# A two-layer transformer kernel: weight columns streamed through TensorE from last to first

## What is computed

```python
# first block
z = rmsnorm(x, attn_norm_g) @ w_in
x = x + concatenate([y_pool, y_attn], -1) @ w_out
up = rmsnorm(x, ffn_norm_g) @ w_up          # 2048 x 11264, then the convolution
x = x + (silu(gate) * val) @ w_down         # 5632 x 2048
# second block
proj = rmsnorm_2(h, attn_norm) @ w_in
qh = rmsnorm_2(c_q, q_norm) @ w_uq;  kv = rmsnorm_2(c_kv, kv_norm) @ w_ukv
mixed = g_a * (y_a @ w_branch_a) + g_b * (y_b @ w_branch_b)
h = h + mixed @ w_out
h = h + (silu(hn @ w_gate) * (hn @ w_up)) @ w_down
return rmsnorm_2(h, final_norm)
```

## Time and profile before

| | |
|---|---|
| median of 3 runs | 2428.22 us |
| the profiled execution | 2428.58 us |
| its span in the profile | 2426.7 us |
| TensorE matmul, busy | 2417.1 us, 11684 instructions |
| TensorE weight load, busy | 2036.5 us |
| VectorE, busy | 1371.2 us |
| ScalarE, busy | 1178.5 us |
| read from memory | 446.02 MB, 185 GB/s over the span |

### The profile page before, as it was taken

The page is one execution under the profiler, slowest core; times in us unless marked ns, Lnnn a source line. Parts: engine busy times, 40 slices in busy tenths (PEclk is TensorE's granted clock), DMA queues, the critical chain, the costliest instruction groups (busy, mean ns, idle before and its releaser), DMA issues.

```text
span 2426.7 us, 31051 instructions
## 1 busy us (share of the span) xinstructions
PE 2417.1 (100%) x11684; PEld 2036.5 (84%) x11684; DVE 1371.2 (57%) x1594; ACT 1178.5 (49%) x1534; POOL 59.8 (2%) x100
## 2 busy tenths in 40 slices
PE   9999999999999999999999999999999999999998
PEld 8788888888888888888888888888888888888887
DVE  5675456777777765445454454665545445454544
ACT  5544445555555544445455544544444444444443
POOL 0000000000000000001120000000000000000000
PEclk9999999999999999999999999999999999999999
DMA  7665456666666655556655556556666666666664
GB/s 249 176 178 167 148 183 182 192 186 185 192 192 179 195 196 190 190 190 186 186 165 174 162 160 184 189 184 189 187 189 188 190 190 189 189 190 207 193 193 155
DMA packets 241049, 449.40 MB, mean 185 GB/s; under 512 B 20100, under 2 KB 26980, under 8 KB 240832
## 3 DMA queue, kind: packets, MB, share of 16 engines
q1 hardware_dynamic: 239952, 445.57, 60.4%
q0 software_dynamic: 624, 2.24, 0.3%
q10 hardware_dynamic: 384, 0.37, 0.0%
HBM read 446.02 MB, written 2.10 MB: 185 GB/s over the span
## 4 chain that ended last, share of the span: by engine, by line
PE 99%; issue 0%; DMA 0%; DVE 0%; ACT 0%; POOLq 0%; POOL 0%; ACTq 0%; DVEq 0%
PE acc L576 25%; PE acc L578 25%; PE acc L577 25%; PE acc L925 7%; PE bank L925 7%; PE bank L928 3%; PE acc L928 3%; PE bank L567 2%; PE bank L749 1%; PE bank L777 0%; PE bank L807 0%; PE bank L726 0%; PE bank L778 0%; PE bank L752 0%; DMA stage<-in_gains 0%
## 5 line engine op out<-in xcount | busy, mean ns | idle before, releaser
L1350 DVE TENSOR_TENSOR w_lo<-w_raw,w_hi 128x1024 fp32r<-128x1024 f32 (+1 forms) x843 | 1027.6, 1221 | 1019.4 <-ACT w_hi L1015 1018.7
L1015 ACT ACTIVATE w_hi<-w_raw 128x1024 fp32r<-128x1024 f32 (+1 forms) x843 | 887.2, 1055 | 1110.9 <-PE acc L578 985.8
L576 PE MATMUL acc<-w_hi,xT 128*128 128x512 f32 (+1 forms) x1532 | 603.4, 394 | 0.0
L578 PE MATMUL acc<-w_hi,xT 128*128 128x512 f32 (+1 forms) x1532 | 595.1, 388 | 0.0
L577 PE MATMUL acc<-w_lo,xT 128*128 128x512 f32 (+1 forms) x1532 | 594.2, 388 | 0.0
L578 PEld LDWEIGHTS acc<-w_hi,xT 128*128 128x128 f32 x1532 | 287.7, 188 | 59.6
L576 PEld LDWEIGHTS acc<-w_hi,xT 128*128 128x128 f32 x1532 | 287.9, 188 | 57.9 <-issue 1.3
L577 PEld LDWEIGHTS acc<-w_lo,xT 128*128 128x128 f32 x1532 | 288.1, 188 | 56.4
L576 PE MATMUL acc<-w_hi,f_hi 128*128 128x512 f32 x688 | 268.3, 390 | 0.0
L578 PE MATMUL acc<-w_hi,f_lo 128*128 128x512 f32 x688 | 267.9, 389 | 0.0
L577 PE MATMUL acc<-w_lo,f_hi 128*128 128x512 f32 x688 | 267.9, 389 | 0.0
(11 more groups left out here) (235 smaller groups left out, 1812.9 us busy)
## 6 DMA issues: line engine op xcount, KB each, us to landing
w_raw<-in_w_up SPq DMA_DIRECT2D x264, 512.0 KB, 3.7
w_raw<-in_w_in SPq DMA_DIRECT2D x199, 512.0 KB, 3.6
w_raw<-in_w_down SPq DMA_DIRECT2D x176, 512.0 KB, 4.2
w_raw<-in_w_gate SPq DMA_DIRECT2D x88, 512.0 KB, 3.6
w_raw<-in_w_out SPq DMA_DIRECT2D x64, 512.0 KB, 3.6
w_raw<-in_w_branch_a SPq DMA_DIRECT2D x16, 512.0 KB, 3.7
w_raw<-in_w_branch_b SPq DMA_DIRECT2D x16, 512.0 KB, 3.8
w_raw<-in_w_in SPq DMA_DIRECT2D x10, 320.0 KB, 3.1
```

The source lines that it names most:

```text
L576: pe.matmul(o, l, w_hi[:, slot, k, 0:width], start=start, stop=False)
L578: last = pe.matmul(o, m, w_hi[:, slot, k, 0:width], start=False, stop=stop)
L1015: act.activation(in_slot(w_hi, slot, width), in_slot(w_raw, slot, width), ACT.Copy).then_inc(w_split_hi, 1)
L1350: dve.tensor_tensor(in_slot(w_lo, slot, width), in_slot(w_raw, slot, width), in_slot(w_hi, slot, width).bitcast(F32), ALU.subtract).then_i ...
```

## The change

The moving operand and the output of every matmul in `columns()` and `last_columns()` are taken through a view with its columns in reverse: the read of the weights begins at the last column and steps by -1, and so does the write to PSUM. Column j of the weights still ends in column j of the bank. Nothing else differs: the same matmuls in the same order with the same stationary operands, semaphores and transfers. `up_turned()`, `first_columns()`, `kw_columns()`, the transposes and the attention products are as they were.

```diff
+            def swept(v):
+
+                return v[:, ::-1]
+
             def columns(c, k, width, operand, start, stop, g):
 
                 hi, lo = operand
                 slot = chunk.now % RING
                 for t in range(NT):
-                    o = acc[g][t][:, 0:width]
+                    o = swept(acc[g][t][:, 0:width])
                     l, m = hi[:, t * P:(t + 1) * P], lo[:, t * P:(t + 1) * P]
-                    pe.matmul(o, l, w_hi[:, slot, k, 0:width], start=start, stop=False)
-                    pe.matmul(o, l, w_lo[:, slot, k, 0:width], start=False, stop=False)
-                    last = pe.matmul(o, m, w_hi[:, slot, k, 0:width], start=False, stop=stop)
+                    h, r = swept(w_hi[:, slot, k, 0:width]), swept(w_lo[:, slot, k, 0:width])
+                    pe.matmul(o, l, h, start=start, stop=False)
+                    pe.matmul(o, l, r, start=False, stop=False)
+                    last = pe.matmul(o, m, h, start=False, stop=stop)
                 return last
 
             def last_columns(t, c, par, ends):
@@
                 kt = (FT // KC - RING + c) * KC
                 for k in range(KC):
                     h, l = f_hi[:, kt + k, t * P:(t + 1) * P], f_lo[:, kt + k, t * P:(t + 1) * P]
-                    pe.matmul(acc[par][t][:], h, w_hi[:, slot, k], start=False, stop=False)
-                    pe.matmul(acc[par][t][:], h, w_lo[:, slot, k], start=False, stop=False)
-                    last = pe.matmul(acc[par][t][:], l, w_hi[:, slot, k], start=False, stop=ends and k == KC - 1)
+                    o, w, r = (swept(v) for v in (acc[par][t][:], w_hi[:, slot, k], w_lo[:, slot, k]))
+                    pe.matmul(o, h, w, start=False, stop=False)
+                    pe.matmul(o, h, r, start=False, stop=False)
+                    last = pe.matmul(o, l, w, start=False, stop=ends and k == KC - 1)
                 return last
```

## The result

The changed kernel takes 2477.14 us (median of 4 runs, 2476.99 to 2477.33) against 2428.2 us before: a ratio of 1.0202, with a 95% interval of 1.0189 to 1.0215. It is 48.9 us slower.

The account below looks back on a forecast made before the run. The prediction took TensorE's end-to-end matmul stream to bound the kernel; 2428.58 + 0 = 2428.6 us, less 0.36 us to the runs' median, gave 2428.2 us. Its own range was 2426 to 2432 us, the stated range 2426 to 4125 us.

Parts of the forecast that it names:

- What bounds the kernel: Whole program: TensorE's matmuls laid end to end, filling 2417.1 of 2426.7 us; the end moves with the swept matmuls' pace.
- the count: Two edited functions: 7884 matmuls of 512 columns at 0.2269 us and 96 of 320 at 0.1467, together 1803 us.
- (a): All engines: no instruction added, removed or moved, no semaphore, transfer or stationary load different; costs nothing.
- (b): Each swept matmul's view: a new first address and step -1, a possible price once per matmul; taken as zero.
- (d): Write of swept matmuls: each column added into PSUM one element below the one before; taken as zero.
- the rule's other reading: Skill's PSUM rule read as one on 8-byte lines: columns 511 and 510 share a line, so the change costs nothing.
- (c): Moving read of swept matmuls: each of 512 columns read one element below the one before; taken as zero.
- the nearest row: Swept matmuls: the present pace of 0.2269 us was taken as nearest to the downward streams, so no change.
- 13 ns a matmul, whatever its width: Swept matmuls: time left beside one column per cycle of 2.4 GHz, claimed equal for 320 and 512 columns.
- bounded that rest from below: Swept matmuls: the rest could shrink from 13.4 to 2.3 ns, giving back 89 us, hence 2340 us.
- Half the rate: Rival, swept read or PSUM add: downward columns taken singly, two cycles each, 4015 to 4122 us; chance 0.37.
- The small price: Rival, each swept matmul: a few cycles for far start or late address turn, eight giving 2455 us; chance 0.08.

Follow-up runs that it names:

- the bench: Kernel with TensorE alone, nothing of the reference, sections of float32r matmuls differing in width, direction and place; 512 columns took 226.7 ns upwards, 233.4 ns with both downwards.
- the table: TensorE alone, 48 matmuls a section, moving and stationary operands each offset 0, 8, ... 56 columns; equal offsets upwards 226.7 to 227.3 ns, all pairs downwards 233.3 to 233.5.
- both benches: Two TensorE-alone kernels, sections of 96 and of 48 matmuls, with the stationary operand shifted by 16 columns against unshifted, read upwards: 233.4 ns in each.

## Why the prediction was wrong

**What bounds the kernel, and the count**: right. TensorE's stream is end to end in both kernels, 7980 matmuls are swept, and the change moved the end by their pace alone. None of the other engines, transfers or waits took part, and the matmuls outside the two functions kept their pace. The ground was a little larger than counted: taken from all starts, the 512-column matmuls had 228.5 ns in the mean before, not 226.9.

**(a) and (b), no instruction moved, no price once per matmul**: right as far as the runs show. The 320-column piece paid nothing, and downward steps inside groups of four paid nothing.

**(d), the write to PSUM**: right, 2427.88 us. The rule of the Trainium skill ("PSUM — Partial Sum Buffer", Specifications), read as one on ascending pairs, would have slowed this kernel; it did not. The downward write keeps to the same lines, so the rule's other reading stands; no run here tests it.

**(c), the read: here it failed.** I took zero because "both streams stay dense" and "two columns that follow each other are as near in memory as they were", and I named the present 0.2269 us as the nearest row. The read measured 6.4 ns on each 512-column matmul. Dense was not enough. What I had set aside as "13 ns a matmul, whatever its width" was the very thing that changed: it was 13.4 ns at 512 columns because moving and stationary operand lie a multiple of 256 bytes apart (the pace fits that row of the bench, and a shift by 256 bytes changed nothing, one by 32 bytes did), and 20.0 ns is about what most other offsets give, and what the downward read gives at all 64 pairs of the table. I had bounded that rest from below, and for raising it had thought only of a fixed price per matmul. Nor is it the same at every width, as I had said: the bench has 16.7 ns at 480 and 504 columns.

**The rivals.** Half the rate, which got 0.37, did not come. Its mechanism, a pace that needs ascending pairs, is excluded by the kernel with groups of four downwards, 2427.85 us. The small price, on 0.08, had the sign; the true price per matmul is 16 cycles of 0.417 ns, twice the largest that I worked out for it (eight cycles, 2455 us), and its mark, 320 columns growing by as many ns, did not show. As a share of the half-rate price, the true one is 49 of 1587 us. That the stated range, 2426 to 4125 us, holds 2477 us is luck: it was stretched for half the rate, and the forecast's own range ended at 2432.

**What stays open.** That the read of the stationary operand takes part is shown for the upward read: its pace depends on the difference of their places, and comes back after 256 bytes. That the two reads hold each other up in the same memory is the likeliest account of it, and is not seen directly. For the downward read the runs show the price and its grain, not its cause: it has no good offset, and no shape of the stationary operand that was tried brought it under 233.3 ns. A stationary operand read the other way round could tell more, and was not tried. Nor do the runs say why 320 columns escape.

No kernel here beats the one before. Upwards at equal offsets is the best that was found; whole blocks of 64 or more columns in reverse order, or columns reversed inside groups of four, are as fast.

## What to carry to other kernels

With float32r, the place of the moving operand against the stationary one, modulo 256 bytes, was worth 2.25% of this TensorE-bound kernel (2427.86 to 2482.34 us): keep both on 256-byte boundaries, and measure a padded tile when a stream of 512-column matmuls takes more than 227 ns each. A reversed view was free where only the output had it, where blocks of 64 columns were reversed as wholes, and where it stayed inside groups of four columns. And when an argument says "nothing changes", look at the part of the measured duration that the model leaves over: it is where a change hides.

## What the runs showed of the hardware

- A float32r matmul of 512 columns takes 226.7 ns from start to start at best and about 233.3 ns at most offsets. The worst pattern tried, downwards inside blocks of 16 columns, takes 266.7 ns. Bfloat16 takes 216 ns at each offset and in each direction that was tried with it.
- "TensorE: Matmul & The Clock Gate" of the Trainium skill (What happens when you issue a matmul) has it that loading the next weights takes no read bandwidth from the running matmul, over two independent ports. For bfloat16 the bench does not speak against it (216 ns with the moving operand at four offsets; the stationary one stayed in place). For float32r a shift of the stationary operand by 64 bytes changed a matmul by 6.7 ns, from 226.7 to 233.4, in both benches.
- "SBUF — State Buffer" of the Trainium skill (Specifications) describes lines of 16 bytes and wants two hits on each. That the order inside a group of four columns is free agrees with it (2427.85 us). That a moving read of every second column takes 229.9 ns for 256 columns, against 120.0 ns for 256 in a row, does not: it has its two hits per line and is nearly half as fast.
